# Query units in halves, six more marked rows, an earlier start of the dense products, and VectorE adding V's fourth bank, in a one-core decoder-layer kernel

## Chip, cores and metric

One core of a Trainium2 chip runs the whole kernel. Times are device microseconds of that core. TensorE, VectorE, ScalarE, GpSimd and SyncE each run their own queue of instructions; SyncE and GpSimd issue most of the transfers, which run on 16 transfer engines.

## What is computed

One layer of a decoder, float32, 256 tokens of 2048 channels: an input projection, a convolution group and a sparse attention group, an output projection, a layer norm, then PEER, a layer of single-neuron experts, and a second layer norm. The change touches PEER alone:

```python
def peer(x, w_q, sub_keys, u_tab, v_tab):        # x: 256 tokens x 2048
    q = (xt @ w_q).reshape(n_tok, 8, 2, 128)     # 8 heads, two half queries each
    s = jnp.einsum('nhcd,hckd->nhck', q, sub_keys)
    s1, i1 = lax.top_k(s[:, :, 0], 16)           # 16 of 128 first keys
    s2, i2 = lax.top_k(s[:, :, 1], 16)           # 16 of 128 second keys
    cand_s = s1[..., :, None] + s2[..., None, :]
    cand_i = i1[..., :, None] * 128 + i2[..., None, :]
    top_s, pos = lax.top_k(cand_s, 16)           # 16 of 16384 experts a head
    gates = softmax(top_s)
    h = gelu(einsum('td,thed->the', x, u_tab[experts]), exact)
    return einsum('the,thed->td', gates * h, v_tab[experts])
```

Each token thus needs 8 x 16 = 128 rows of U and of V, 8 KB each.

## The kernel before

**Expert rows.** Tokens lie on 128 partitions, in two tiles of 128. Work goes in 256 numbered *rows* (`ALL`): row s is expert slot s mod 128 of token tile s div 128, a different expert for every partition. GpSimd gathers it (line 512) into one of six places in SBUF, from row 42 (`WIDER_AT`) of seven; a place holds 8 KB of U and 8 KB of V for each partition. Then, row by row:

- VectorE, `dot` (line 1825): the product of the U half with x1 and its sum;
- ScalarE, `gelu` (lines 1266 to 1290): the gelu, the weight (gelu times gate), and the V half times the weight, in two operations of 1024 columns;
- TensorE, `add_turned` (line 880): sixteen transposing products of 128 x 128 that add the scaled V half, turned, into four banks of PSUM; then `y_done` frees the place. From row 248 (`TOKEN_AT`) on, `add_row` (line 891) adds it unturned with a diagonal matrix, in products of 128 x 512, after `turn_back` has turned the banks back.

GpSimd waits for `dots_done` of the row that had the place before it refills the U half, and for `y_done` before the V half.

**Marked rows and dense keys.** Most tokens share some first keys. `popularity` counts them per head, `count` (TensorE, at row 24, `COUNT_AT`) sums over tokens, and `choose` (VectorE, at row 25) takes the 24 most frequent. For these the kernel computes all 128 experts of the key for all tokens: *dense U* is 24 units of 1 MB of U (`dense_part`, line 951), each in four parts, spread over rows 40 to 104 by `DENSE_SLOT`; *dense V* is 24 units of 1 MB of V (`v_dense`, line 993), spread over rows 166 (`VALUES_AT`) to 239 by `VALUE_SLOT`. Between the two, rows 109 to 165 carry the sixteen *chunks* that spread the gates over the dense experts, with two-input operations on VectorE (lines 1850 to 1866).

`mark` (VectorE) gives a row's tokens that use a dense key an id out of bounds, so that the gather skips them; `divide` splits their gates between `row_gate` and `gate`. Rows 32 to 255 (`SPLIT` on) are marked. A marked row is two gathers, one of U halves, then, one row later in GpSimd's queue, one of V halves with the partitions' two halves exchanged. Rows 0 to 31 are not marked and come in one gather of 16 KB a partition. The last two rows have their own ids.

**Query units.** The first heads' queries are made before row 0. The other twelve (`LATER`) half queries come from weight units of 1 MB that SyncE loads (three buffers), each multiplied in three parts (`QUERY_PARTS`, `unit_part`, line 919) in rows 0 to 35, sixteen products of 128 x 256 a unit. ScalarE copies, TensorE scores against the sub-keys (`unit_score`, line 928), ScalarE copies again, VectorE counts the popular keys in the order of `UNIT_ORDER`. Each (tile, head) in `RANKED` takes seven rows (`PACE`) of VectorE steps: the top 16 of both key sets, of their sums, the experts, the gates. The place that is added at row 42 lies where the query weights were, so GpSimd waits there for `unit_scored`.

The order on each engine is written out by the row number in one loop per engine; each engine runs through its own list and waits on semaphores.

Of the kernel before, what the change touches and what calls it, by code (L numbers as in the profile page):

```python
# [11 lines left out]
ALU = mybir.AluOpType  # L12
# [40 lines left out]
WIDER_AT = 42  # L53
# [8 lines left out]
QUERY_PARTS = 3  # L62
# [7 lines left out]
DENSE_ROWS = 65  # L70
DENSE_SLOT = [LATER * QUERY_PARTS + 4 + DENSE_ROWS * m // (DENSE * PARTS) for m in range(DENSE * PARTS)]
# [19 lines left out]
ORDER = BEFORE + [(0, 2), (1, 1), (1, 0), (0, 3)] + RANKED[6:]  # L91
# [15 lines left out]
SPLIT = len(BEFORE) * TOP  # L107
# [4 lines left out]
def layer(nc, xT, x_tok, w_stream, w_kw, w_sub, conv_p, cln, bucket1h, rel_bias,  # L112
          b_out, ln1_col, ln_rows, uv_tab, dense_u, out):
    with ExitStack() as ctx:  # L114
# [180 lines left out]
        key_of = [at_early(f"key_of{c}", [P, TI, SLOTS], 4096 + 1024 * c) for c in range(2)]  # L295
        row_gate = at_early("row_gate", [P, TI, SLOTS], 6144)
# [78 lines left out]
        gates_done, weight_done, parked = sem("gates_done"), sem("weight_done"), sem("parked")  # L375
# [74 lines left out]
        def _(pool):  # L450
# [64 lines left out]
            def place_read(s):  # L515

                pool.wait_ge(y_done, BEFORE_IT[s] + 1)

# [7 lines left out]
            for s in range(ALL):  # L526
                k = PLACE[s]
                i, j = ROW_OF[s]
                if s == 0:
                    pool.wait_ge(first_picked, 1)  # L530
                elif s == 1:
                    pool.wait_ge(picked, 1)
                elif j % TOP == 0 and s < SPLIT:
                    pool.wait_ge(picked, ORDER.index((i, j // TOP)) + 1)
                elif j % TOP == 0:
                    pool.wait_ge(turn_ready, ORDER.index((i, j // TOP)) + 1 - len(BEFORE))
# [27 lines left out]
        def _(pe):  # L564
# [333 lines left out]
            def turn_back(i, banks):  # L898

                for n in banks:  # L900
# [59 lines left out]
            def ids_turn():  # L960

                pe.wait_ge(turn_ready, TI * PH - len(BEFORE))
                pe.wait_ge(gates_done, TI * PH)
# [45 lines left out]
            for s in range(ALL - TAIL):  # L1009
# [40 lines left out]
        def _(act):  # L1050
# [211 lines left out]
            def gelu(s):  # L1262
# [3 lines left out]
                act.activation(dots[:, s:s + 1], dots[:, s:s + 1], ACT.Gelu).then_inc(gelu_done, 1)  # L1266
                if j % TOP == 0:
                    act.wait_ge(gates_done, ORDER.index((i, j // TOP)) + 1)
                act.wait_ge(gelu_done, s + 1)
                if split(s):  # L1270
                    if j % TOP == 0:
                        act.wait_ge(turn_ready, ORDER.index((i, j // TOP)) + 1 - len(BEFORE))
# [39 lines left out]
            def dense_copy(v):  # L1312
# [4 lines left out]
                if v >= EXTRA:  # L1317
                    act.wait_ge(*((picked, v - EXTRA + 1) if RANKED[v - EXTRA] in BEFORE else (turn_ready, ORDER.index(RANKED[v - EXTRA]) + 1 - len(BEFORE))))
# [27 lines left out]
            for s in range(3, ALL):  # L1346
                gelu(s)
                if s % QUERY_PARTS == 0 and 1 <= s // QUERY_PARTS <= LATER:
                    unit_copy(s // QUERY_PARTS - 1)
                if s % QUERY_PARTS == 2 and 1 <= s // QUERY_PARTS <= LATER:  # L1350
                    unit_keys(s // QUERY_PARTS - 1)
# [26 lines left out]
        def _(dve):  # L1378
# [374 lines left out]
            def mark(i, h):  # L1753

                q = i * PH + h
                first, second = (t[:, i, h * TOP:(h + 1) * TOP] for t in key_of)
                dve.scalar_tensor_tensor(out=posf[0][:, :], in0=first, scalar=float(PK), in1=second, op0=ALU.mult, op1=ALU.add)
                wide = [P, TOP, DENSE]
                match = cand_both[:, 0:TOP * DENSE].rearrange("p (r j) -> p r j", j=DENSE)
                link(dve.tensor_tensor(match, first.rearrange("p (r o) -> p r o", o=1).to_broadcast(wide),  # L1760
                                       dense_key[:, :].rearrange("p (o j) -> p o j", o=1).to_broadcast(wide), ALU.is_equal))
                link(dve.tensor_reduce(of_dense[:, :], match, AX.X, ALU.add))
# [5 lines left out]
                link(dve.scalar_tensor_tensor(out=posf[1][:, :], in0=of_dense[:, :], scalar=float(SKIP),  # L1768
                                              in1=posf[0][:, :], op0=ALU.mult, op1=ALU.add))
                turn_ids(i, h)  # L1770

            def divide(i, h):

                g, r = (t[:, i, h * TOP:(h + 1) * TOP] for t in (gate, row_gate))
                link(dve.scalar_tensor_tensor(out=r, in0=of_dense[:, :], scalar=0.5, in1=g, op0=ALU.is_lt, op1=ALU.mult))
                dve.tensor_tensor(g, g, of_dense[:, :], ALU.mult).then_inc(gates_done, 1)
# [26 lines left out]
            def gates_out(r):  # L1803
# [7 lines left out]
                if (i, h) in BEFORE:  # L1811
                    link(dve.tensor_copy(row_gate[:, i, h * TOP:(h + 1) * TOP], g))
                    dve.memset(g, 0.0).then_inc(gates_done, 1)
                elif r >= 4:
                    divide(i, h)
# [11 lines left out]

            def turn_identity():
# [4 lines left out]
            def turn_ids(i, h):  # L1833

                c = i * SLOTS + h * TOP - SPLIT
                cols = slice(c, c + TOP)
                dve.tensor_scalar(u_id[:, cols], posf[1][:, :], 2.0, None, ALU.mult)
                dve.tensor_scalar(v_id[HALF:P, cols], posf[1][0:HALF, :], 2.0, 1.0, ALU.mult, ALU.add)
                dve.tensor_scalar(v_id[0:HALF, cols], posf[1][HALF:P, :], 2.0, 1.0, ALU.mult, ALU.add).then_inc(turn_ready, 1)
                dve.wait_ge(turn_ready, ORDER.index((i, h)) + 1 - len(BEFORE))  # L1840

# [59 lines left out]
            for s in range(ALL - TAIL):  # L1901
                dot(s)
                if s == 0:
# [6 lines left out]
                if r < TI * PH:  # L1910
                    if t == 2:
                        keys_top(r)
                    if t == 3:
                        sums_top(r)
                    if t == 5:
                        hits()
                    if t == 6:
# [13 lines left out]
                for h in range(2, PH):  # L1931
                    u = UNIT_ORDER.index(2 * h)
                    if s == QUERY_PARTS * u + QUERY_PARTS + 3:
# [121 lines left out]
```

## Time and profile before

| | us |
|---|---|
| median of three runs | 1606.35 (1605.69 to 1611.81) |
| the profiled execution | 1601.73 |
| its span | 1599.9 |
| first dot, last dot | 436.4, 1578.4 |
| VectorE busy / TensorE busy / ScalarE busy / GpSimd busy | 1212.1 / 1477.1 / 989.9 / 801.9 |

| from - to, us | what runs |
|---|---|
| 0 - 436 | projections, attention, convolution, first layer norm |
| 453 - 617 | rows 3 to 31, unmarked, with the query units |
| 617 - 654 | rows 32 to 39, marked, with the last query unit |
| 654 - 950 | rows 40 to 104, with dense U |
| 950 - 1199 | rows 105 to 165; the chunks from 1000 us or so |
| 1199 - 1526 | rows 166 to 239, with dense V |
| 1526 - 1600 | last rows, second layer norm, output |

The busy time of TensorE is modelled for pipelined products, so near its full share it does not tell how far the engine is from its limit. The share of the transfer engines is the time that packets took, over sixteen engines; it can pass 1.

### The profile page before, as it was taken

To read this page: it belongs to the slowest core of one execution; us is meant where nothing else is said; L and a number is where in the kernel's file an instruction comes from. 1 tells how busy PE (TensorE), PEld (TensorE's weight loads), DVE (VectorE), ACT (ScalarE), POOL (GpSimd) and SP (SyncE) were. 2 spreads that over 40 slices of the span, in tenths; PEclk is the share of its full clock that TensorE was granted. 3 is DMA by queue.
4 is the path that set the end of the run, shared out by engine and by line. 5 is a ranking of instruction groups with operands and counts; after the bars stand their busy time and mean duration, and the time that the engine had idled before them with its cause. 6 is when DMAs were issued, how large, how long until landed. Compare 5 with 4: busy or idle time off the path is not lost. (4 is left out here: it accounts for less than half of the span.)

```text
span 1599.9 us, 27076 instructions
## 1 busy us (share of the span) xinstructions
PE 1477.1 (92%) x10428; PEld 1343.4 (84%) x10428; DVE 1212.1 (76%) x2091; ACT 989.9 (62%) x1632; POOL 801.9 (50%) x515
## 2 busy tenths in 40 slices
PE   9999999999998779899999997888879989989986
PEld 8999899988887668787899987878868989989973
DVE  5689999775776689978889888888965445445586
ACT  5433345553456557767778677777767657556692
POOL 0000110100123335665667668888888867546883
PEclk9999999999999999999999999888889999999998
DMA  6575544376599999999999999899999999999995
GB/s 258 178 247 182 197 170 154 137 293 233 224 426 426 427 427 418 399 415 394 382 408 418 410 390 368 289 376 384 378 357 394 416 416 412 413 412 403 413 360 198
DMA packets 92977, 543.99 MB, mean 340 GB/s; under 512 B 28274, under 2 KB 28946, under 8 KB 32018
## 3 DMA queue, kind: packets, MB, share of 16 engines
q0 software_dynamic: 71296, 405.11, 63.7%
q1 hardware_dynamic: 20884, 137.00, 22.5%
q8 instruction: 79, 1.29, 0.3%
q14 instruction: 46, 0.38, 0.1%
q10 hardware_dynamic: 672, 0.21, 0.1%
HBM read 682.45 MB, written 4.19 MB: 429 GB/s over the span
## 5 line engine op out<-in xcount | busy, mean ns | idle before, releaser
L512 POOL DMA_INDIRECT uv_row<-in_uv_tab,turned x444 | 710.0, 1599 | 266.1 <-issue 112.2
L1825 DVE CUSTOM_DVE_ANT_0 uv_row<-uv_row,x 128x2048 f32<-128x2048 f32 x256 | 586.8, 2292 | 240.2 <-DMA uv_row<-in_uv_tab,turned 195.1
L1290 ACT ACTIVATE uv_row<-uv_row,turned 128x1024 f32<-128x1024 f32 x432 | 473.1, 1142 | 211.0 <-DMA uv_row<-in_uv_tab,turned 208.4
L880 PE MATMUL psum<-popular,uv_row 128*128 128x128 f32 x3456 | 456.9, 286 | 75.6 <-ACT uv_row L1290 75.2
L880 PEld LDWEIGHTS psum<-popular,uv_row 128*128 128x128 f32 x3456 | 404.0, 148 | 117.0 <-ACT uv_row L1290 108.6
L571 PE MATMUL psum<-xT_hi,w_hi 128*128 128x256 f32 x640 | 183.1, 286 | 3.2 <-DVE w_lo L1410 3.1
L993 PE MATMUL psum<-scratch,dense_unit 128*128 128x128 f32 x1536 | 183.8, 275 | 0.0
L572 PE MATMUL psum<-xT_lo,w_hi 128*128 128x256 f32 x640 | 181.2, 283 | 0.0
L573 PE MATMUL psum<-xT_hi,w_lo 128*128 128x256 f32 x640 | 181.2, 283 | 0.0
L993 PEld LDWEIGHTS psum<-scratch,dense_unit 128*128 128x128 f32 x1536 | 177.6, 192 | 0.0
L951 PE MATMUL psum<-x1T,dense_unit 128*128 128x256 f32 x768 | 176.6, 379 | 0.0
L1065 ACT ACTIVATE w_hi<-w_raw 128x2048 fp32r<-128x2048 f32 x62 | 118.7, 1915 | 85.6 <-DMA w_raw<-in_w_stream 85.6
L1410 DVE TENSOR_TENSOR w_lo<-w_raw,w_hi 128x2048 fp32r<-128x2048 f32 x62 | 141.6, 2286 | 28.7 <-ACT w_hi L1065 27.8
L951 PEld LDWEIGHTS psum<-x1T,dense_unit 128*128 128x128 f32 x768 | 141.0, 190 | 16.3
L1275 ACT ACTIVATE turned<-dots,row_gate 64x1 f32<-64x1 f32 x444 | 129.8, 292 | 11.0 <-issue 0.4
L571 PEld LDWEIGHTS psum<-xT_hi,w_hi 128*128 128x128 f32 x640 | 122.8, 192 | 7.0 <-issue 3.1
L572 PEld LDWEIGHTS psum<-xT_lo,w_hi 128*128 128x128 f32 x640 | 122.9, 192 | 0.1
L573 PEld LDWEIGHTS psum<-xT_hi,w_lo 128*128 128x128 f32 x640 | 122.8, 192 | 0.0
L512 POOL DMA_INDIRECT uv_row<-in_uv_tab,eid x32 | 52.3, 1634 | 114.1 <-PE psum L880 96.7
L1266 ACT ACTIVATE dots<-dots 128x1 f32<-128x1 f32 x256 | 48.9, 191 | 67.3 <-DVE dots L1825 67.0
L880 PE MATMUL psum<-ident,uv_row 128*128 128x128 f32 x512 | 66.9, 281 | 24.6 <-ACT uv_row L1290 24.6
L880 PEld LDWEIGHTS psum<-ident,uv_row 128*128 128x128 f32 x512 | 57.4, 144 | 34.9 <-ACT uv_row L1290 34.0
(281 smaller groups left out, 1712.8 us busy)
## 6 DMA issues: line engine op xcount, KB each, us to landing
w_raw<-in_w_stream SPq DMA_DIRECT2D x63, 1024.0 KB, 4.8
dense_unit<-in_dense_u SPq DMA_DIRECT2D x24, 1024.0 KB, 8.9
dense_unit<-in_uv_tab SPq DMA_DIRECT2D x24, 1024.0 KB, 9.3
wq_first<-in_w_stream SPq DMA_DIRECT2D x8, 1024.0 KB, 12.6
uv_row<-in_uv_tab,turned POOLq DMA_INDIRECT x444, 19.1
wq_third<-in_w_stream SPq DMA_DIRECT2D x4, 1024.0 KB, 11.8
xT_raw<-in_xT SPq DMA_DIRECT2D x4, 512.0 KB, 5.4
turned_rows<-dist_row POOLq DMA_DIRECT2D x1, 2048.0 KB, 14.3
```

Of the source, the lines that this page charges most:

```text
L512: pool.indirect_dma_start(dst, None, tab, bass.IndirectOffsetOnAxis(ap=ids, axis=0), bounds_check=tab.shape[0] - 1, oob_is_err=False).then ...
L571: pe.matmul(dst, a[0], b[0], start=first, stop=False)
L572: pe.matmul(dst, a[0], b[1], start=False, stop=False)
L573: return pe.matmul(dst, a[1], b[0], start=False, stop=last)
L880: last = pe.matmul(bank(i, b // 4)[:, b % 4 * P:(b % 4 + 1) * P], row[k][:, D + b * P:D + (b + 1) * P], order[:, :], is_transpose=True, st ...
L951: last = pe.matmul(side[v % 2][:, 0:S], w[:, c, :], x1T[:, c, :], start=c == 0, stop=c == KC - 1)
L993: last = pe.matmul(bank(i, n)[:, b % 4 * P:(b % 4 + 1) * P], dense_unit[v % 2][:, b * P:(b + 1) * P], mixed[:, v, i * P:(i + 1) * P], star ...
L1065: act.activation(w_hi[k], w_raw[k], ACT.Copy).then_inc(hi_done, 1)
L1275: whole = act.activation(weight_turned[to, c:c + 1], dots[of, s:s + 1], ACT.Identity, scale=row_gate[of, i, j:j + 1])
L1290: act.activation(v, v, ACT.Identity, scale=w).then_inc(scaled, 1)
L1410: dve.tensor_tensor(w_lo[k], w_raw[k], w_hi[k].bitcast(F32), ALU.subtract).then_inc(lo_dve, 1)
L1825: dve.tensor_tensor_reduce(row[k][:, 0:D], row[k][:, 0:D], x1[:, ROW_OF[s][0], :], 1.0, 0.0, ALU.mult, ALU.add, dots[:, s:s + 1]).then_inc ...
```

## The change

- `QUERY_PARTS` 3 to 2: query units in halves, in rows 1 to 24; the calls that belong to them move accordingly, and `unit_score` now stands ahead of `unit_part` in TensorE's row. `WIDER_AT` 42 to 36.
- `COUNT_AT` 24 to 18: keys are chosen at row 19; `UNIT_ORDER` brings the units that count forward. The chosen keys are the same.
- `SPLIT` 32 to 26: the last six slots of head (0, 1) are marked as well; `mark` and `divide` take a first slot j. The marks of (0, 1), (1, 0), (0, 2) follow at rows 19, 20 and 21.
- `DENSE_ROWS` 65 to 78, start at row 27 instead of 40: dense U ends at row 104 as before.
- In rows 166 to 247 (`ADDED`) TensorE adds twelve blocks, not sixteen, ScalarE scales 1024 + 512 columns, and VectorE adds the fourth bank, weighted, into `y_last` in SBUF (`add_last`), behind the next row's dot. GpSimd waits for it as well before it refills the place. TensorE adds `y_last` once, at row 248.

```diff
-WIDER_AT = 42
+WIDER_AT = 36
...
-QUERY_PARTS = 3
+QUERY_PARTS = 2
...
-DENSE_ROWS = 65
-DENSE_SLOT = [LATER * QUERY_PARTS + 4 + DENSE_ROWS * m // (DENSE * PARTS) for m in range(DENSE * PARTS)]
+DENSE_ROWS = 78
+DENSE_SLOT = [LATER * QUERY_PARTS + 3 + DENSE_ROWS * m // (DENSE * PARTS) for m in range(DENSE * PARTS)]
...
-UNIT_ORDER = [4, 5, 6, 8, 10, 12, 14, 7, 9, 11, 13, 15]
+UNIT_ORDER = [4, 6, 8, 10, 5, 12, 14, 7, 9, 11, 13, 15]
-COUNT_AT = 24
+COUNT_AT = 18
...
-SPLIT = len(BEFORE) * TOP
+LATE = 10
+ADDED = range(VALUES_AT, TOKEN_AT)
+SPLIT = TOP + LATE
...
             def place_read(s):
                 pool.wait_ge(y_done, BEFORE_IT[s] + 1)
+                if BEFORE_IT[s] in ADDED:
+                    pool.wait_ge(y_last_done, ADDED.index(BEFORE_IT[s]) + 1)
...
-                    for b in range(8 * half, 8 * half + 8):
+                    for b in range(8 * half, 12 if half and s in ADDED else 8 * half + 8):
...
+                    if i == 1 and n == 3:
+                        pe.wait_ge(y_last_done, len(ADDED))
+                        last = pe.matmul(bank(1, 3), ident_turned[:, :], y_last[:, :], start=False, stop=True, skip_group_check=True)
...
-                if s < LATER * QUERY_PARTS:
-                    unit_part(s // QUERY_PARTS, s % QUERY_PARTS)
-                if s >= QUERY_PARTS + 1 and s % QUERY_PARTS == 1 and s // QUERY_PARTS <= LATER:
-                    unit_score(s // QUERY_PARTS - 1)
+                if s >= 4 and s % QUERY_PARTS == 0 and (s - 4) // QUERY_PARTS < LATER:
+                    unit_score((s - 4) // QUERY_PARTS)
+                if 1 <= s <= LATER * QUERY_PARTS:
+                    unit_part((s - 1) // QUERY_PARTS, (s - 1) % QUERY_PARTS)
...
-                    v = row[PLACE[s]][:, D + half * DC:D + (half + 1) * DC]
+                    v = row[PLACE[s]][:, D + half * DC:D + (DC + 512 if half and s in ADDED else (half + 1) * DC)]
...
+            def add_last(s):
+                k, n, c = PLACE[s], ADDED.index(s), split_col(s)
+                dve.wait_ge(weight_done, s + 1)
+                dve.wait_ge(v_half_in[k], v_half_from[k] + 16 * SPLIT_USES[s])
+                if n:
+                    dve.wait_ge(y_last_done, n)
+                dve.scalar_tensor_tensor(out=y_last[:, :], in0=row[k][:, D + 3 * 512:2 * D], scalar=weight_turned[:, c:c + 1],
+                                         in1=y_last[:, :], op0=ALU.mult, op1=ALU.add).then_inc(y_last_done, 1)
...
                 dot(s)
+                if s == VALUES_AT:
+                    link(dve.memset(y_last[:, :], 0.0))
+                if s - 1 in ADDED:
+                    add_last(s - 1)
...
                 if s == CHOSEN_AT:
                     choose()
                     turn_identity()
+                    mark(0, 1, LATE)
+                    divide(0, 1, LATE)
+                if s == CHOSEN_AT + 1:
+                    mark(1, 0)
+                    divide(1, 0)
+                if s == CHOSEN_AT + 2:
                     mark(0, 2)
                     divide(0, 2)
-                if s == CHOSEN_AT + 3:
-                    mark(1, 0)
-                    divide(1, 0)
```

## Rows read from the trace of the kernel before

**Rows 1.** The page: rate in 40 slices, and the group of ScalarE's scaling.
```profile
GB/s 258 178 247 182 197 170 154 137 293 233 224 426 426 427 427 418 399 415 394 382 408 418 410 390 368 289 376 384 378 357 394 416 416 412 413 412 403 413 360 198
...
L1290 ACT ACTIVATE uv_row<-uv_row,turned 128x1024 f32<-128x1024 f32 x432 | 473.1, 1142 | 211.0 <-DMA uv_row<-in_uv_tab,turned 208.4
```

**Rows 2.** Table by stage: length, five engines' busy us, TensorE clock, DMA share, GB/s.
```profile
453.00:617.00 164.00, 138.16 (x851) 119.97 (x851) 120.28 (x301) 95.23 (x151) 52.90 (x33) 0.99 1.01 426
617.00:654.00 37.00, 32.84 (x222) 29.11 (x221) 34.29 (x79) 28.59 (x51) 20.28 (x14) 1.00 1.00 407
654.00:950.00 296.00, 283.44 (x1789) 254.16 (x1790) 257.13 (x611) 221.80 (x377) 196.35 (x137) 0.99 1.00 404
...
1040.00:1199.00 159.00, 133.69 (x957) 124.03 (x958) 128.81 (x127) 111.88 (x196) 135.83 (x77) 0.86 0.97 373
1199.00:1526.00 327.00, 313.05 (x2703) 301.76 (x2702) 170.40 (x148) 215.79 (x378) 233.44 (x156) 0.99 1.01 410
```

**Rows 3.** The same table for shorter stretches (columns PE, PEld, DVE, ACT, POOL).
```profile
740.00:800.00 60.00, 58.45 (x379) 53.19 (x380) 54.67 (x131) 47.66 (x82) 39.23 (x27) 1.00 0.98 382
820.00:900.00 80.00, 80.00 (x523) 73.51 (x522) 71.86 (x177) 64.28 (x109) 54.46 (x39) 1.00 1.01 416
980.00:1040.00 60.00, 54.58 (x428) 51.21 (x427) 53.01 (x55) 44.94 (x77) 52.70 (x24) 0.92 0.86 303
...
520.00:580.00 60.00, 48.91 (x298) 40.93 (x296) 41.39 (x96) 33.73 (x54) 19.93 (x11) 1.00 1.01 427
```

**Rows 4.** Queue 0: whole kernel, 654 to 950 us, 1199 to 1526 us.
```profile
q0 software_dynamic: 71296, 405.11, 63.7%
...
q0 software_dynamic: 19484, 96.19, 81.1%
...
q0 software_dynamic: 22075, 110.50, 83.6%
```

**Rows 5.** Waits, 654 to 950 us: total us, times, longest.
```profile
POOL uv_row L512 <- PE psum L880: 44.1, 29, 3.2
...
ACT scratch L1319 <- PE psum L951: 29.4, 12, 4.1
...
DVE gsum L1808 <- ACT gate L1260: 18.6, 7, 3.6
...
DVE uv_row L1825 <- DMA uv_row<-in_uv_tab,turned: 9.3, 5, 3.1
```

**Rows 6.** Timeline of TensorE, 760 to 800 us: start, us, line.
```profile
773.42 3.62 PE L951 MATMUL psum<-x1T,dense_unit 128*128 128x256 f32 x16
776.88 1.91 PE L880 MATMUL psum<-popular,uv_row 128*128 128x128 f32 x16
778.62 1.89 PE L951 MATMUL psum<-x1T,dense_unit 128*128 128x256 f32 x8
```

**Rows 7.** Waits, 1199 to 1526 us.
```profile
DVE uv_row L1825 <- DMA uv_row<-in_uv_tab,turned: 156.5, 73, 4.8
...
POOL uv_row L512 <- PE psum L880: 42.8, 27, 3.4
...
POOL uv_row L512 <- DVE dots L1825: 11.3, 5, 2.8
```

**Rows 8.** Line 512, gathers issued in three stretches: ns min/median/max.
```profile
L512 POOL DMA_INDIRECT uv_row<-in_uv_tab,turned x137: 984/991/3071, 653.7 to 947.5; - x137
...
L512 POOL DMA_INDIRECT uv_row<-in_uv_tab,turned x156: 984/991/3088, 1198.7 to 1525.8; - x156
...
L512 POOL DMA_INDIRECT uv_row<-in_uv_tab,turned x11: 1686/2965/3049, 998.9 to 1026.1; - x11
```

**Rows 9.** Line 1889, VectorE's last-norm operation, ns min/median/max.
```profile
L1889 DVE SCALAR_TENSOR_TENSOR x<-x,rstd,ln_rows_sb x8: 746/746/753, 1558.8 to 1595.9; 128x512 f32<-128x512 f32 x8
```

**Rows 10.** Timelines of TensorE and GpSimd near the end.
```profile
1563.67 24.20 PE L891 MATMUL psum<-uv_row,scratch 128*128 128x512 f32 x56
...
1556.82 2.69 POOL L512 DMA_INDIRECT uv_row<-in_uv_tab,turned  x1 [0.31 <-issue]
```

More of the change, by code:

```diff
@@ L374, in layer @@
             sem(n) for n in ("chunk_ready", "chunk_done", "chunk_mixed", "v_dense_done"))
-        gates_done, weight_done, parked = sem("gates_done"), sem("weight_done"), sem("parked")
+        gates_done, weight_done, parked, y_last_done = (sem(n) for n in ("gates_done", "weight_done", "parked", "y_last_done"))
         row2_done, row2_copied = sem("row2_done"), sem("row2_copied")
@@ L532, in _ @@
                     pool.wait_ge(picked, 1)
-                elif j % TOP == 0 and s < SPLIT:
-                    pool.wait_ge(picked, ORDER.index((i, j // TOP)) + 1)
+                elif s == TOP:
+                    pool.wait_ge(picked, 2)
+                elif s == SPLIT:
+                    pool.wait_ge(turn_ready, 1)
                 elif j % TOP == 0:
-                    pool.wait_ge(turn_ready, ORDER.index((i, j // TOP)) + 1 - len(BEFORE))
+                    pool.wait_ge(turn_ready, RANKED.index((i, j // TOP)))
                 if k == 4 and s < PLACES:
@@ L1266, in gelu @@
                 act.activation(dots[:, s:s + 1], dots[:, s:s + 1], ACT.Gelu).then_inc(gelu_done, 1)
+                r = RANKED.index((i, j // TOP))
                 if j % TOP == 0:
-                    act.wait_ge(gates_done, ORDER.index((i, j // TOP)) + 1)
+                    act.wait_ge(gates_done, r + 1 if r < 2 else r + 2)
+                elif s == SPLIT:
+                    act.wait_ge(gates_done, 3)
                 act.wait_ge(gelu_done, s + 1)
                 if split(s):
-                    if j % TOP == 0:
-                        act.wait_ge(turn_ready, ORDER.index((i, j // TOP)) + 1 - len(BEFORE))
+                    if s == SPLIT or j % TOP == 0:
+                        act.wait_ge(turn_ready, max(r, 1))
                     c = split_col(s)
@@ L1317, in dense_copy @@
                 if v >= EXTRA:
-                    act.wait_ge(*((picked, v - EXTRA + 1) if RANKED[v - EXTRA] in BEFORE else (turn_ready, ORDER.index(RANKED[v - EXTRA]) + 1 - len(BEFORE))))
+                    r = v - EXTRA
+                    act.wait_ge(*((picked, r + 1) if RANKED[r] in BEFORE else (turn_ready, r)))
                 act.activation(mixed[:, BLOCK_OF[v], :], side[v % 2][:, 0:S], ACT.Gelu).then_inc(dense_copied, 1)
@@ L1347, in _ @@
                 gelu(s)
[L1348 to L1351, printed above, removed]
+                if s >= 3 and s % QUERY_PARTS == 1 and (s - 3) // QUERY_PARTS < LATER:
+                    unit_copy((s - 3) // QUERY_PARTS)
+                if s >= 5 and s % QUERY_PARTS == 1 and (s - 5) // QUERY_PARTS < LATER:
+                    unit_keys((s - 5) // QUERY_PARTS)
                 r, t = s // PACE + 1, s % PACE
@@ L1751, in experts, with mark @@
                                              in1=pick[1][:, j:], op0=ALU.mult, op1=ALU.add).then_inc(picked, 1)
-            def mark(i, h):
+            def mark(i, h, j=0):
                 q = i * PH + h
[L1756 to L1759, printed above, removed]
+                n = TOP - j
+                first, second = (t[:, i, h * TOP + j:(h + 1) * TOP] for t in key_of)
+                ids, of = posf[0][:, 0:n], of_dense[:, 0:n]
+                dve.scalar_tensor_tensor(out=ids, in0=first, scalar=float(PK), in1=second, op0=ALU.mult, op1=ALU.add)
+                wide = [P, n, DENSE]
+                match = cand_both[:, 0:n * DENSE].rearrange("p (r j) -> p r j", j=DENSE)
                 link(dve.tensor_tensor(match, first.rearrange("p (r o) -> p r o", o=1).to_broadcast(wide),
                                        dense_key[:, :].rearrange("p (o j) -> p o j", o=1).to_broadcast(wide), ALU.is_equal))
-                link(dve.tensor_reduce(of_dense[:, :], match, AX.X, ALU.add))
+                link(dve.tensor_reduce(of, match, AX.X, ALU.add))
                 if q == TI * PH - 1:
@@ L1767, in mark, with divide @@
                         link(dve.tensor_scalar(last_id[:, a, :], last_f[:, :], 2.0, float(a), ALU.mult, ALU.add))
[L1768 to L1776, printed above, removed]
+                link(dve.scalar_tensor_tensor(out=posf[1][:, 0:n], in0=of, scalar=float(SKIP), in1=ids, op0=ALU.mult, op1=ALU.add))
+                turn_ids(q * TOP + j - SPLIT, n, RANKED.index((i, h)))
+            def divide(i, h, j=0):
+                g, r = (t[:, i, h * TOP + j:(h + 1) * TOP] for t in (gate, row_gate))
+                of = of_dense[:, 0:TOP - j]
+                if j:
+                    dve.memset(gate[:, i, h * TOP:h * TOP + j], 0.0)
+                link(dve.scalar_tensor_tensor(out=r, in0=of, scalar=0.5, in1=g, op0=ALU.is_lt, op1=ALU.mult))
+                dve.tensor_tensor(g, g, of, ALU.mult).then_inc(gates_done, 1)
             def popularity(i, h):
@@ L1831, in turn_identity, with turn_ids @@
                 link(dve.tensor_copy(ident_turned[:, HALF:P], ident[:, 0:HALF]))
[L1833 to L1840, printed above, removed]
+            def turn_ids(c, n, ready):
+                cols, ids = slice(c, c + n), posf[1]
+                dve.tensor_scalar(u_id[:, cols], ids[:, 0:n], 2.0, None, ALU.mult)
+                dve.tensor_scalar(v_id[HALF:P, cols], ids[0:HALF, 0:n], 2.0, 1.0, ALU.mult, ALU.add)
+                dve.tensor_scalar(v_id[0:HALF, cols], ids[HALF:P, 0:n], 2.0, 1.0, ALU.mult, ALU.add).then_inc(turn_ready, 1)
+                dve.wait_ge(turn_ready, ready)
             def chunk_keys(c, half):
@@ L1914, in _ @@
                         sums_top(r)
+                    if t == 4:
+                        hits()
                     if t == 5:
-                        hits()
-                    if t == 6:
                         experts(r)
```

13 lines of the change are left out of this document (8 added, 5 removed).

## The prediction, made before the result was known

> **What bounds the kernel now.** I read the rate in the page's 40 us slices first [rows 1]. From 440 us to 1560 us, the whole stage of the expert rows, it shows where the transfers are short of their best: 427 GB/s at first, 418 to 382 in the middle, 289 in the slice at 1000 us, 357 to 394 until 1240, then 403 to 416. A table by stage [rows 2] adds how busy the transfer engines were: DMA share 1.01, 1.00, 1.00, 0.97, 1.01. So the gather stage is bound by transfers, and a change there is worth what it takes from the bytes or gives back of the rate, and nothing else.
>
> The rate needs a yardstick, so I cut out stretches in which nothing disturbs the transfers [rows 3]: whole 16 KB rows run at 427 GB/s (520 to 580 us), half rows at 416 (820 to 900). Beside them stand 382 GB/s (740 to 800), where TensorE is busy 58.5 of 60 us, and 303 GB/s (980 to 1040), where GpSimd is busy 52.7 of 60 us issuing the gathers. Then I asked who waits for whom while dense U runs [rows 5]: VectorE waits for a landing in only 9.3 of 296 us, GpSimd waits 44.1 us for TensorE to free a place, and ScalarE waits 29.4 us for a dense product. With VectorE busy 257.1 and TensorE 283.4 of 296 us [rows 2], three resources are nearly full at once there. While dense V runs it is different: VectorE waits for landings 156.5 of 327 us [rows 7] and is busy only 170.4 [rows 2].
>
> **The change, part by part.**
>
> *Six more rows marked.* Rows 26 to 31 become two half gathers that skip the tokens of the 24 dense keys. A whole row is 128 x 16 KB = 2.10 MB, at 427 GB/s 4.91 us. For a marked row I divide what queue 0 moved [rows 4] by the gathers issued meanwhile [rows 8], two to a row: 96.19 MB / 68.5 = 1.40 MB while U runs, 110.50 / 78 = 1.42 while V runs. From above, all of queue 0's 405.1 MB less 32 whole rows (67.1 MB) over 224 marked rows is 1.51 MB, and that still holds other transfers. I take 1.45 MB, 69% of a row, 3.49 us at 416 GB/s. Saved 1.42 us a row, times 6: **8.5 us**; at 1.40 and 1.51 MB it is 9.2 and 7.7. What a single head skips may lie outside both; I allow 7 to 11. Six more gathers on GpSimd (0.99 to 3.1 us each [rows 8]) lie beside the transfers: that engine is busy 52.9 of 164 us before row 32 [rows 2]. One more marking on VectorE and one memset, some 2.5 us by my estimate from the short operations of that stage, and all first markings now stand in rows 19 to 21 instead of 25 and 28. VectorE is busy 120.3 of 164 us there, and five more rows are in flight behind the one it works on. I take 0; if the cover is gone, 3 us once.
>
> *Query units in halves.* The same 12 MB of weights and the same products, in 24 rows instead of 36. Transfers: 4.91 us for the row plus half a unit (0.52 MB, 1.23 us) make 6.1 us a row. TensorE: eight products instead of 5.3. Sixteen records take 1.73 us more than eight, so a product of two records takes 0.43 us, and sixteen transposes are followed by the next work after 1.74 us [rows 6]; with 0.2 for the scores that is 3.5 + 1.7 + 0.2 = 5.4 us. Transfers stay the longer, and the bytes move earlier, not away: 0, at worst 2 us of missed overlap. GpSimd's wait for the last unit's scores moves with the seventh place from row 42 to 36; the scores are then made at TensorE's row 26, ten rows ahead of that gather, so the wait should vanish. The stage at 617 to 654 us, which holds it, still ran at DMA share 1.00 and 407 GB/s [rows 2], so at most 1 us comes back.
>
> *Dense U from row 27 to 104 instead of 40 to 104.* The bytes stay. Per row TensorE now has 96 / 78 = 1.23 quarter units instead of 1.48. A quarter is 8 records, 1.73 us [rows 6], so 1.74 + 2.14 = 3.9 us a row instead of 1.74 + 2.57 = 4.3. The transfers of such a row: 3.49 us plus 24 / 78 of a 1.05 MB unit (0.78 us) = 4.3 us, where they were 4.4. TensorE is then 0.4 us clear of them instead of 0.1, and what it cost can come back: the stage moved 404 GB/s x 296 us = 119.6 MB, at 416 GB/s 287.5 us, so 8.5 us were lost. But VectorE stays: its 257.1 us busy and 18.6 us waiting for the gates' exponentials [rows 5] are 4.2 us a row. I take half: **4 us**, between 0 and 8.5. Behind row 105 nothing moves: the same chunks in the same rows, with GpSimd held between VectorE's operations as now (135.8 of 159 us busy [rows 2]).
>
> *V's fourth bank on VectorE, rows 166 to 247.* TensorE loses 4 of 16 transposes (0.44 us a row), ScalarE scales 1536 columns instead of two times 1024, which take 1.14 us each [rows 1] (some 0.55 us less). VectorE gains one 128x512 operation; the nearest row has the same shape and both inputs in SBUF, 0.75 us [rows 9]. 82 x 0.75 = 61 us on VectorE, of which some 75 rows in the stage: 170 + 56 = 226 of 327 us. Its waits for landings (156 us) take that in. The new wait stands behind a dot: the weight and the V half of the row before. What is queued behind it is the next dot, whose U half is issued after that V half, so it would not have run earlier; GpSimd waits additionally for the sum before it refills a V place. The relief on TensorE is off the path: the stage moves 410 GB/s, its middle slices 416 to 412 [rows 1, 2], 3 us at most. I take 0, from -3 to +8 (below).
>
> *The end.* TensorE's last chain is 56 records in 24.2 us from 1563.7 us on [rows 10], 0.43 us a record; the product that adds the VectorE sum is 2 more, +0.9 us on the path. It starts behind ScalarE's scaling of row 247 (now 0.55 less) and sixteen transposes (now 0.4 less). VectorE meanwhile runs dots back to back with GpSimd's gathers tied to them (2.69 us each [rows 10]); seven additions of 0.75 us push these by up to 5 us, of which I put about 3 down as covered, since ScalarE too must finish those rows first. I take **+1 us**, -1 to +4.
>
> Sum: -8.5 - 4 + 0 + 1 = **-11.5 us**. The profiled execution took 1601.7 us (a span of 1599.9 and 1.8 around it), so 1590.2. The median of the three runs is 1606.35 (one was 1611.8), 0.3% above it; on that scale 1594.9, so I forecast **1595 us**, -0.7%. A measurement of this kernel can tell about 0.5%, 8 us, from no change: the marked rows alone are about that much, which is why the sign of the small terms matters.
>
> **A rule that speaks against it.** When a gather is issued while nothing on VectorE stands in its way it takes 0.99 us; between 1000 and 1028 us, where dots and two-input operations follow each other, eleven took 1.69 to 3.05, median 2.97, and the rate fell to 303 GB/s [rows 3, 8]. The Trainium skill (SBUF — State Buffer, "SBUF: two separate sides") states it: VectorE and GpSimd share a port pair that is locked for a whole instruction, and a VectorE operation with two SBUF inputs takes it against a GpSimd operation that reads SBUF. The trace agrees. The new addition has two SBUF inputs.
>
> **Rivals.**
>
> 1. *Slower: GpSimd becomes the bound while dense V runs.* Each gather may have to wait out the new 0.75 us. GpSimd has 42.8 + 11.3 = 54 us of waits for places in 327 us [rows 7], 0.7 us a row. One such wait a row (61 us) is just hidden; from there on each further 0.1 us costs 8 us. Price: if the stage falls to the 373 GB/s of the chunk stage [rows 2], 134 MB take 359 us, +32, in all 1627; at 390 GB/s +17 (344 us), 1612. Against it: VectorE would be busy 69% of this stage, and 81% in the chunk stage; it idles over a microsecond a row, and an undisturbed gather needs 1.0. Chance 0.10.
>
> 2. *VectorE holds dense U's stage.* It has 276 us of work and waits in 296; with the rows from 27 on as fast as 4.2 us it would be full, so no rate comes back, the marking burst costs 3, and the end costs 2: -8.5 + 5 = -3.5, 1603. For it: only 9.3 us of waiting for landings. Against: the gate wait is itself a wait for ScalarE, which waited 29.4 us for dense products. Chance 0.22.
>
> 3. *All of the rate comes back.* TensorE's relief restores 416 GB/s while U runs and 3 us while V runs: -8.5 - 8.5 - 3 = -20, 1586. Chance 0.13.
>
> 4. *The marking does not shorten anything*, since the transfers wait for places before row 32 already: then only the 4 us remain and the end costs its 1: 1603. The share of 1.01 at 426 GB/s [rows 2] speaks against it. Chance 0.05.
>
> The forecast's own case, 1590 to 1600, has 0.50. The range takes in rival 3 and rivals 2 and 4 and leaves out the slow one and the far ends: 1585 to 1607. Faster by over 0.5% (below 1598.3): the forecast's case but for its upper edge (0.46) and rival 3 with its further end, 0.13, and a little of rival 2, 0.05: 0.64. Within 0.5%: the upper edge of the forecast, most of rival 2, rival 4 and the mildest of rival 1, 0.27. Slower: 0.09.
>
> **What would show it.** After the change, rows 26 to 31 should land a microsecond or more apart faster than rows 3 to 25, queue 0 should carry some 401 MB (6 x 0.65 less), the stage of dense U should run at 408 GB/s or more with TensorE busy below 90%, and GpSimd should have no wait for the scores near row 36. While dense V runs the rate should be 405 to 415 GB/s, with VectorE's wait for landings down to about 100 us and gathers whose median stays near 1 us. Wrong would be: rate there below 400 with GpSimd never waiting for a place (rival 1); dense U at 404 or less with VectorE above 90% busy (rival 2); TensorE's last chain starting later against the last landing than now.

## The result and the profile after

The changed kernel takes 1600.5 us (median of 15 runs), the one before 1608.1 in the same sessions: ratio **0.9945, interval 0.9929 to 0.9961**, -8.8 us by the ratio. Forecast were 1595 us and -11.5. Ratios leave out executions that took over 1.5% more than the fastest of their kernel: one of `e2_v_alone` (1670 us), one of `g1_later_and_40` (2858 us) and one of the kernel before (2436 us). A single execution moves by several microseconds (1593 to 1605 for the changed kernel, 1603 to 1614 for the other), so two profiles alone don't show this difference: the profiled spans are 1600.8 and 1599.9 us, and already row 0 starts 2.7 us later in the profile after. So I compare lengths from dot to dot within the stage, over several variants.

| us between dots of rows | 3-24 | 24-32 | 32-40 | 40-105 | 105-166 | 166-240 | 240 to end |
|---|---|---|---|---|---|---|---|
| before | 124.3 | 44.3 | 32.2 | 296.6 | 248.8 | 326.8 | 73.9 |
| after | 130.7 | 37.4 | 34.7 | 290.4 | 251.2 | 326.0 | 74.5 |

Rows 24 to 32 and 40 to 105 are shorter; rows 3 to 24 give 6.4 us back. Such a length is not yet a gain or a loss: a stage also gets shorter when more of its bytes were moved before its first dot. Rate times length tells the two apart. These are the rows of the stage table from the dot of row 3 to that of row 105 and from row 40 to row 105, first of the kernel before, then of the changed one:

```profile
453.30:950.50 497.20, 454.64 (x2864) 403.50 (x2863) 411.87 (x990) 346.13 (x579) 269.54 (x183) 0.99 1.01 411
654.00:950.50 296.50, 283.94 (x1793) 254.66 (x1794) 257.56 (x613) 222.30 (x377) 196.35 (x137) 0.99 1.00 404
...
456.00:949.20 493.20, 455.40 (x2871) 405.26 (x2869) 413.21 (x1000) 347.51 (x581) 272.71 (x188) 0.99 1.00 410
658.80:949.20 290.40, 264.54 (x1705) 234.51 (x1703) 255.10 (x606) 221.63 (x371) 188.58 (x131) 0.99 1.00 402
```

Rows 40 to 105 took 6 us less because 3 MB less were moved in them (404 GB/s x 296.5 us = 119.8 MB, 402 x 290.4 = 116.7), not because the rate rose. From row 3 to row 105 the rate is the same too, and 4 us are gone with 2 MB.

The stage table of the changed kernel, for the stretches that answer to [rows 2] (rows 3 to 31, 32 to 39, 40 to 104, most of the chunks, dense V; columns as there):

```profile
456.00:624.00 168.00, 159.98 (x981) 143.42 (x980) 126.73 (x319) 100.73 (x168) 59.86 (x42) 0.98 1.01 424
624.00:659.00 35.00, 31.08 (x191) 27.54 (x190) 31.55 (x77) 25.32 (x45) 24.48 (x17) 0.95 1.02 416
659.00:949.00 290.00, 264.34 (x1703) 234.31 (x1701) 254.87 (x605) 221.35 (x369) 188.38 (x131) 0.99 1.00 402
1040.00:1200.00 160.00, 135.64 (x960) 124.94 (x958) 128.15 (x127) 110.50 (x194) 137.14 (x76) 0.86 0.96 365
1200.00:1526.00 326.00, 286.14 (x2391) 274.56 (x2392) 220.93 (x222) 184.65 (x378) 236.10 (x153) 0.97 1.01 408
```

TensorE fell from 283.4 of 296 us to 264.3 of 290 while U runs, and yet the rate is 402 GB/s, no better than 404 before. The waits of that stretch, which answer to [rows 5], point to the reason:

```profile
POOL uv_row L514 <- PE psum L886: 33.4, 17, 3.6
ACT dots L1275 <- DVE dots L1845: 27.4, 22, 3.2
POOL uv_row L514 <- DVE dots L1845: 26.3, 9, 3.6
...
DVE gsum L1825 <- ACT gate L1269: 20.1, 8, 4.3
ACT scratch L1332 <- PE psum L960: 7.4, 8, 2.0
...
DVE uv_row L1845 <- DMA uv_row<-in_uv_tab,turned: 0.9, 1, 0.9
```

VectorE waits 0.9 us for landings in 290 us, where it was 9.3. ScalarE now waits for VectorE's dots (27.4 us, before 1.4) and hardly for dense products (7.4, before 29.4). VectorE does not wait for rows, then: the data is there. What it waits for is the exponential of the gates, 20.1 us in 8 waits.

While V runs the waits answer to [rows 7]:

```profile
ACT uv_row L1302 <- DMA uv_row<-in_uv_tab,turned: 136.0, 70, 5.2
DVE uv_row L1845 <- DMA uv_row<-in_uv_tab,turned: 74.8, 63, 3.5
...
POOL uv_row L514 <- PE psum L886: 40.9, 26, 3.5
...
DVE y_last L1855 <- issue: 21.7, 17, 2.3
...
POOL uv_row L514 <- DVE y_last L1855: 3.9, 6, 2.4
```

VectorE's wait for landings fell from 156.5 to 74.8 us, and 21.7 us more pass idle before the additions; in all it is idle 105 of 326 us, where it was 157 of 327. That took the additions in. GpSimd still waits for places, and its gathers of the stage took 1.54 us in the mean, 1.51 before. Queue 0 carries 3.1 MB less, and the addition costs what its nearest row said [rows 4, 9]:

```profile
q0 software_dynamic: 72160, 401.97, 63.6%
...
L1855 DVE SCALAR_TENSOR_TENSOR y_last<-uv_row,turned,y_last x82: 740/747/773, 1207.0 to 1558.6; 128x512 f32<-128x512 f32 x82
```

### The profile page after: what moved, and what is told of

It is laid out like the page before. It is cut to its first block, busy times and chain, and to the rows that moved or that the text cites. A ratio compares the mean times of both kernels' runs of the same rounds, so it can differ in the third digit from the quotient of the medians.

```text
span 1600.8 us, 26707 instructions
## 1 busy us (share of the span) xinstructions
PE 1456.6 (91%) x10102; PEld 1322.7 (83%) x10102; DVE 1269.8 (79%) x2183; ACT 959.7 (60%) x1638; POOL 811.0 (51%) x521
## 4 chain that ended last, share of the span: by engine, by line
DMA 24%; DVE 17%; PE 6%; issue 6%; ACT 5%; POOL 4%; POOLq 0%; DVEq 0%; ACTq 0%
DMA uv_row<-in_uv_tab,turned 24%; DVE uv_row L1845 10%; POOL uv_row L514 4%; PE psum L886 3%; ACT uv_row L1302 3%; PE psum L897 1%; PE psum L1002 1%; ACT L1269 1%; PE psum L989 1%; DVE scratch L1675 0%; DVE first_key L1879 0%; ACT turned L1287 0%; DVE key_of L1759 0%; DVE idx L1681 0%; DVE idx L1674 0%
## 5 line engine op out<-in xcount | busy, mean ns | idle before, releaser
L514 POOL DMA_INDIRECT uv_row<-in_uv_tab,turned x456 | 729.8, 1600 | 273.6 <-issue 121.1
L1302 ACT ACTIVATE uv_row<-uv_row,turned 128x1024 f32<-128x1024 f32 (+1 forms) x444 | 451.1, 1063 | 220.8 <-DMA uv_row<-in_uv_tab,turned 216.5
L886 PE MATMUL psum<-popular,uv_row 128*128 128x128 f32 x3224 | 435.8, 289 | 117.7 <-ACT uv_row L1302 116.8
L886 PEld LDWEIGHTS psum<-popular,uv_row 128*128 128x128 f32 x3224 | 380.2, 148 | 163.6 <-ACT uv_row L1302 155.7
L1002 PE MATMUL psum<-scratch,dense_unit 128*128 128x128 f32 x1536 | 188.7, 280 | 0.0
L1002 PEld LDWEIGHTS psum<-scratch,dense_unit 128*128 128x128 f32 x1536 | 182.8, 197 | 0.0
L960 PE MATMUL psum<-x1T,dense_unit 128*128 128x256 f32 x768 | 180.1, 381 | 0.0
L514 POOL DMA_INDIRECT uv_row<-in_uv_tab,eid x26 | 38.7, 1490 | 98.2 <-PE psum L886 81.0
L1495 DVE SCALAR_TENSOR_TENSOR scratch<-glu_sb,conv_sb,scratch 128x256 f32<-128x256 f32 x203 | 82.6, 473 | 0.0
L487 POOL TENSOR_TENSOR scratch<-scratch,convT 128x256 f32<-128x256 f32 x6 | 16.5, 2745 | 130.3 <-DVE convT L1499 130.3
```

What stands on the lines that cost most here:

```text
L514: pool.indirect_dma_start(dst, None, tab, bass.IndirectOffsetOnAxis(ap=ids, axis=0), bounds_check=tab.shape[0] - 1, oob_is_err=False).then ...
L960: last = pe.matmul(side[v % 2][:, 0:S], w[:, c, :], x1T[:, c, :], start=c == 0, stop=c == KC - 1)
L1002: last = pe.matmul(bank(i, n)[:, b % 4 * P:(b % 4 + 1) * P], dense_unit[v % 2][:, b * P:(b + 1) * P], mixed[:, v, i * P:(i + 1) * P], star ...
```

## The experiments

All ratios are against the kernel before, run on the same chip in the same session. Stage lengths are from one profile each. Rows 40 to 105 repeat within 2 us (290.4 to 292.1 in the four profiles with the changed kernel's work there: `after`, `e1_no_v`, `e3_six_whole`, `f5_add_twice`). Behind row 105 the scatter is larger: rows 105 to 166, where no two kernels differ, took 243.7 to 254.7 us, rows 166 to 240 took 325.8 to 334.9.

**The parts.** Four kernels take one part out, or do one alone.

*Without V's bank* (`e1_no_v`; the memset and the product that adds `y_last` go with it):

```diff
-ADDED = range(VALUES_AT, TOKEN_AT)
+ADDED = range(0)
```

> The changed kernel with V's fourth bank given back to TensorE and ScalarE; the rest of the change stays. The changed kernel stands at 0.9945 of the one before (-8.8 us). Theory of the forecast (the stage of dense V is bound by transfers, the bank costs 1 us at the end): 0.994, 1598 to 1600 us beside 1608. Rival 1 (VectorE's addition holds up the gathers and costs several us in rows 166 to 247): 0.991 or less. Rival 3 (TensorE's relief gives back rate while V runs): 0.996 or more.

Measured 0.9956 (0.9936 to 0.9975). *V's bank alone, on the kernel before* (`e2_v_alone`: `ADDED`, `add_last`, the twelve blocks, the shorter scaling, the wait in `place_read`, the memset and the last product, nothing else):

> The kernel before with V's fourth bank on VectorE and nothing else. Theory of the forecast: 1.000 to 1.001 (0 to +2 us), the stage of rows 166 to 239 within 2 us of 327. Rival 1: 1.003 or more, with gathers issued later and the rate below 405 GB/s. Rival 3: 0.998, the stage 3 us shorter.

Measured 0.9973 (0.9954 to 0.9991). So the bank is worth -1.8 us in the one pair, with an error of 4, and -4.3 in the other, with an error of 3. The stage of dense V itself doesn't show it above its scatter: 326.8 us before and 332.2 with the bank alone, 330.3 without it and 326.0 with it in the changed kernel. The first pair is the forecast's value within its error, the second is at rival 3's; neither leaves room for rival 1.

*The six rows whole again* (`e3_six_whole`; keys still chosen at row 19):

```diff
-SPLIT = TOP + LATE
+SPLIT = 2 * TOP
...
-                    mark(0, 1, LATE)
-                    divide(0, 1, LATE)
+                    dve.sem_inc(turn_ready, 1)
+                    dve.memset(gate[:, 0, TOP:2 * TOP], 0.0).then_inc(gates_done, 1)
```

> The changed kernel with rows 26 to 31 gathered whole and unmarked as before; keys are still chosen at row 19 and dense U still starts at row 27. Theory of the forecast (bytes at the transfers' rate: 8.5 us): 0.9945 + 0.0053 = 0.9998, some 1608 us, queue 0 back at 405 MB. Rival (transfers wait for places there, marks shorten nothing): 0.994 to 0.996.

Measured 1.0020 (0.9995 to 1.0045), 1607.6 us, queue 0 at 405.11 MB. The marking carries the gain: 0.0075 between the two, 12 us, with an error of some 5. Rows 24 to 32 took 44.3 us here at 423 GB/s and 37.4 in the changed kernel at 416, that is 18.7 and 15.6 MB; the 3.1 MB are what queue 0 lost. Over all variants profiled those rows took 44.3 to 45.8 us unmarked (five) and 34.6 to 37.6 marked (nine), some 8 us apart, near the term of the sum. Without the marking the rest of the change is no gain.

*Dense U from row 40 again* (`e4_dense_from_40`):

```diff
-DENSE_ROWS = 78
-DENSE_SLOT = [LATER * QUERY_PARTS + 3 + DENSE_ROWS * m // (DENSE * PARTS) for m in range(DENSE * PARTS)]
+DENSE_ROWS = 65
+DENSE_SLOT = [LATER * QUERY_PARTS + 16 + DENSE_ROWS * m // (DENSE * PARTS) for m in range(DENSE * PARTS)]
```

> The changed kernel with dense U spread over rows 40 to 104 again; the marked rows, the query units in halves and V's bank stay. Theory of the forecast (4 us of rate come back by the spreading, between 0 and 8.5): 0.997, some 1604 us, with 380 to 405 GB/s while U runs. Rival 2 (VectorE holds that stage, spreading gives nothing): 0.9945, no different from the changed kernel.

Measured 0.9941 (0.9917 to 0.9964): the spreading brings nothing that shows; a gain of 4 us would lie at the edge of the error. Rows 40 to 105 took 286.9 us with all 24 units inside, 290.4 with the spread, both at 402 GB/s. Its row of the stage table and two of its waits:

```profile
657.00:944.00 287.00, 280.49 (x1780) 254.42 (x1781) 255.21 (x606) 221.05 (x374) 183.05 (x130) 0.99 1.00 402
```
```profile
ACT scratch L1332 <- PE psum L960: 39.5, 16, 4.1
...
DVE gsum L1825 <- ACT gate L1269: 21.3, 9, 3.2
```

TensorE is as full as it was before the change, ScalarE waits for its products as before, and the rate is the same 402 GB/s. TensorE was late, and that cost no rate.

*Query units in halves alone* (`f1_halves_alone`, on the kernel before: `QUERY_PARTS = 2` with the calls that move, `WIDER_AT = 36`; keys still at row 25, dense U from row 40):

> The kernel before with the query units in halves and the seventh place from row 36, nothing else: keys chosen at row 25, rows 0 to 31 whole, dense U from row 40. The traces so far show two sides of this. Rows 3 to 24 took 130 to 131 us with units in halves and 124 to 125 in thirds; rows 40 to 105 took 287 to 292 us with them and 295 to 297 in thirds, where GpSimd stood 8.9 us at row 42 and was then only 2 to 3 rows ahead. New theory (the stage of dense U is bound by VectorE when its rows are there, and the stall is what made it wait): both show, +6 and -6 to -9, total 0.996 to 1.001. Forecast's theory (bytes only move, the stall costs at most 1 us): 1.000 to 1.001, rows 40 to 105 unchanged at 295 us or more.

Measured 1.0015 (0.9995 to 1.0035). Rows 3 to 24 took 129.6 us (124.3 in thirds), rows 40 to 105 290.9 (296.6). The two are one thing seen twice, as the rows of the stage table from row 3 to row 105 and from row 40 to row 105 show (those of the kernel before are above):

```profile
452.90:950.00 497.10, 457.61 (x2864) 411.66 (x2863) 411.58 (x990) 346.35 (x579) 267.75 (x183) 0.97 1.00 412
659.10:950.00 290.90, 281.34 (x1793) 254.40 (x1794) 257.27 (x613) 223.11 (x380) 190.70 (x132) 0.99 1.00 403
```

Rows 40 to 105 ran at 403 GB/s, 404 in the kernel before: the 5.6 us that they are shorter are some 2.5 MB that were moved ahead of row 40, where they cost as much. Up to row 105 both kernels take 497 us.

The stall at row 42 goes with the same edit. In the kernel before GpSimd stands there 8.9 us, with the place whose memory the query weights hold, and is then, from row 37 to row 48, only 3 or 4 rows ahead of VectorE, where `f1_halves_alone` has 5 or 6. Its wait in the stretch 628 to 665 us, and the same stretch in `f1_halves_alone`:

```profile
POOL uv_row L512 <- PE psum L928: 8.9, 1, 8.9
```
```profile
POOL uv_row L512 <- issue: 5.8, 19, 0.3
POOL uv_row L512 <- PE psum L880: 0.3, 1, 0.3
```

The lost lead looks dear in rows 40 to 105 and is not: it is bytes that come later, and the 497 us show no price for the stall. No run moves the place alone.

**Who is the bound from row 40 to 105?** Two kernels add work there, one takes a wait away. `f2_vector_more` and `f3_tensor_more` add, per row:

```diff
+                if 40 <= s < 105:
+                    link(dve.tensor_reduce(dense_count[:, 0:1], iota_f[:, :], AX.X, ALU.add))
```
```diff
+                if 40 <= s < 105:
+                    pe.matmul(ps[0][:, 0:S], x1T[:, 0, 0:P], x1T[:, 0, :], start=True, stop=True)
```

> The changed kernel with one more VectorE operation (a sum over 256 columns, some 0.42 us, its result unused) in each of rows 40 to 104. New theory (VectorE is the bound there): nearly its whole price shows, 65 x 0.45 = 29 us, 1625 to 1630 us, rows 40 to 105 in 315 to 320 us. Forecast's theory (transfers and TensorE are the bound): under 8 us.

> The changed kernel with one more product of 128 x 256 (0.43 us, its result unused) on TensorE in each of rows 40 to 104, 28 us of work. New theory (VectorE is the bound): 0 to 6 us. If TensorE still decides there: 20 us or more.

Measured 1.0080 (1.0050 to 1.0111) and 0.9973 (0.9946 to 1.0000), against 0.9945 without either. Their rows of the stage table, VectorE's first:

```profile
655.00:962.00 307.00, 274.13 (x1697) 239.94 (x1695) 279.12 (x670) 221.11 (x370) 205.34 (x131) 0.97 0.97 383
```
```profile
654.00:945.00 291.00, 284.06 (x1819) 256.21 (x1818) 254.80 (x605) 220.07 (x370) 189.18 (x131) 1.00 1.00 400
```

24 us more of VectorE's work lower the rate from 402 to 383 GB/s and make the stage 17 us longer (290.4 to 307.5 us from dot to dot) and the kernel 22 us slower, with an error of some 5; 20 us more of TensorE's make the stage 1 us longer and the kernel 4.5 us slower with about the same error. So VectorE is the bound of the changed kernel there, though not for its full price: I had written 29 us.

*The gates taken up one row later* (`f4_gates_later`), so that ScalarE's exponential is done when VectorE comes for it:

```diff
-                if t == 0 and 1 <= r - 1 < TI * PH:
+                if (t == 1 if 4 <= r - 1 < TI * PH - 1 else t == 0) and 1 <= r - 1 < TI * PH:
```

> The changed kernel with VectorE taking up the gates of the fifth to fifteenth ranked head one row later, so that it no longer waits for ScalarE's exponential (20.1 us in 8 waits between rows 40 and 105). New theory (VectorE is the bound): rows 40 to 105 fall from 290 us towards 119 MB at 416 GB/s, 280 to 284 us, total 0.989 to 0.992. Forecast's theory (bound by transfers): within 2 us of the changed kernel, 0.9945.

Measured 0.9924 (0.9896 to 0.9952), rows 40 to 105 in 285.3 us. Its waits and its stage row:

```profile
656.00:942.00 286.00, 262.53 (x1677) 232.24 (x1676) 255.74 (x608) 219.66 (x371) 203.01 (x130) 0.99 1.01 406
```
```profile
DVE uv_row L1845 <- DMA uv_row<-in_uv_tab,turned: 16.3, 12, 3.6
...
DVE gsum L1825 <- ACT gate L1269: 1.3, 2, 1.1
```

19 us of waiting for ScalarE are gone, 5 us come off the stage, at 406 GB/s instead of 402, and 15 us turn up as waits for landings: right behind VectorE stand the transfers. The step 0.9945 to 0.9924 lies within the two intervals; the stage's length and the waits are what show it.

The same edit on the kernel before (`h1_before_gates_later`; there the gates of head (1, 1) are divided with another head's marks, because those are made in between, so the output is wrong; the work is the same):

> The kernel before with VectorE taking up the gates of the fifth to fifteenth ranked head one row later, nothing else. There VectorE waited 18.6 us for the exponentials in rows 40 to 105, but TensorE was busy 283 of 296 us and held places back 44 us. If VectorE alone were the bound, it gains as in the changed kernel: rows 40 to 105 at 288 to 291 us, ratio 0.995 to 0.998. If TensorE is as late as VectorE there (dense U in 65 rows and the stall at row 42), within 2 us: 0.999 to 1.001.

Measured 0.9982 (0.9965 to 0.9999), but rows 40 to 105 stayed at 296.6 us. VectorE's wait for the gates fell from 18.6 to 7.4 us and its wait for landings rose from 9.3 to 18.6. So in the kernel before the rows themselves were late in that stage, VectorE was not its bound alone, and what the total gained I can't place.

**Does the addition hold up the gathers?** `f5_add_twice` makes it twice, the first time with weight 0:

```diff
+                link(dve.scalar_tensor_tensor(out=y_last[:, :], in0=row[k][:, D + 3 * 512:2 * D], scalar=0.0,
+                                              in1=y_last[:, :], op0=ALU.mult, op1=ALU.add))
```

> The changed kernel with VectorE's addition of V's fourth bank made twice in rows 166 to 247 (the extra one with weight 0, same operands), 82 x 0.75 = 61 us more work with two SBUF inputs. In the changed kernel VectorE still waits 74.8 us for landings there, and only 6 gathers met the addition (mean 1.36 us instead of 0.99). Forecast's theory (landings' waits take it in, the gathers are hardly held): rows 166 to 239 in 326 to 336 us, total at most +6 us on the changed kernel, ratio 0.995 to 0.998. Rival 1 (the port lock makes GpSimd the bound): 15 us or more, ratio 1.003 or more, GpSimd without a wait for a place, rate below 400 GB/s.

Measured 0.9975 (0.9951 to 0.9999), rows 166 to 240 in 328.6 us. The stage, and two waits:

```profile
1193.00:1522.00 329.00, 288.56 (x2393) 277.49 (x2392) 268.87 (x296) 184.23 (x377) 221.15 (x154) 0.96 1.01 410
```
```profile
POOL uv_row L514 <- PE psum L886: 55.3, 33, 4.8
...
DVE uv_row L1845 <- DMA uv_row<-in_uv_tab,turned: 37.7, 33, 3.7
```

Twice the additions, and GpSimd still waits for places, 55.3 us instead of 40.9, at the same 410 GB/s; a gather of the stage took 1.44 us in the mean, 1.54 in the changed kernel. Rows 240 to 248 took 34.4 us instead of 30.0 (27.3 without the addition): most of what the total lost.

**The fastest.** `g1_later_and_40` joins the later gates and dense U from row 40; `h2_best_no_v` takes V's bank out of it.

> The changed kernel with VectorE taking up the gates one row later (0.9924 by itself) and dense U spread over rows 40 to 104 again (0.9941 by itself). If in rows 40 to 105 both VectorE's waits and the transfers are near the bound: spreading dense U from row 27 keeps 13 rows' share of bytes out of that stage, so this should be no better than the gates alone: rows 40 to 105 in 287 to 292 us, but rows 3 to 40 shorter by some 3 us; 0.991 to 0.995. If the early bytes only cost: 0.990 or less.

> The fastest variant so far (gates one row later, dense U from row 40; 0.9903) with V's fourth bank given back to TensorE and ScalarE. The two pairs so far put the bank on VectorE at -1.8 us (changed kernel) and -4.3 us (alone on the kernel before), each within 3 to 4 us. If that gain is real: ratio 0.992 to 0.993. If it is nothing: 0.990 to 0.991.

Measured 0.9903 (0.9872 to 0.9934), 1594.6 us, and 0.9909 (0.9889 to 0.9928), 1593.9 us. By the ratio both beat the kernel before by some 15 us, by the medians by 10 and 13, and they are the fastest measured; from the changed kernel (0.9929 to 0.9961) the second is just clear, the first overlaps it by a hair. Against `f4_gates_later` alone, rows 3 to 40 took 197.9 us instead of 201.1 in the first, rows 40 to 105 287.8 instead of 285.3, and rows 3 to 105 485.7 instead of 486.4: spreading dense U from row 27 moves bytes from the one stretch to the other and neither gains nor clearly costs. V's bank is -1 us in this pair, with an error of some 6. Over the three pairs, weighted by their errors, it is 3 us gained, give or take 2; only the pair on the kernel before (0.9954 to 0.9991) is clear of nothing by itself, and narrowly.

## Why the prediction came out as it did

- **Six more rows marked, -8.5 us: right in mechanism, oversized in bytes.** Rows 24 to 32 are 7 to 8 us shorter, and taking the marks back costs 12 us with an error of 5. Queue 0 lost 3.14 MB, 0.52 a row, where I had 0.65, so these six rows skip only a quarter of their tokens. That is 6.8 us by the rates of [rows 3], and the 3.1 MB between `e3_six_whole` and the changed kernel in rows 24 to 32 took 6.9. What the 12 us hold beyond that, if not chance, I can't assign. The sign that I had set, rows 26 to 31 a microsecond closer to each other than rows 3 to 25, told nothing: these six took 28.4 us and the 23 ahead of them 139.7, but 29.0 and 139.5 in the kernel before, where they were not marked.
- **Query units in halves, 0: right.** The forecast was that "the bytes move earlier, not away", and they did: rows 3 to 24 took 5 to 6 us longer, rows 40 to 105 as much less, and up to row 105 the time is the same 497 us. The wait at row 42 vanished as forecast, and "at most 1 us comes back" holds too.
- **Dense U from row 27, -4 us: wrong.** The failed step is "at 416 GB/s 287.5 us, so 8.5 us were lost", with TensorE as the one who lost them, and half of the gap taken as gain without a row behind it. TensorE busy 264.3 of 290 us or 280.5 of 287, the rate was 402 GB/s both times, where 408 or more was the sign I had set. In the changed kernel VectorE freed places no faster; its 276 us of work and gate waits stood in my own text as rival 2. In the kernel before the runs name no single bound: 11 us less of gate waits left the stage at 296.6 us. Relief for TensorE moved a wait from one engine to another (29.4 us of ScalarE's to 7.4, and 1.4 us for dots to 27.4). The premise ahead of it, that the whole gather stage is bound by transfers because their share reads 1.00, failed with it: in rows 40 to 105 the share is 1.00 too, and VectorE's operations set the time.
- **V's bank, 0 us: right within its range, -3 to +8; the pairs say some 3 us gained.** The added work went where the wait for landings was, 156.5 to 74.8 us (forecast: about 100). Rival 1 fell: its condition was one wait of 0.75 us a row; 7 of 153 gathers of the stage were issued while an addition ran, and took 1.30 us in the mean.
- **The end, +1 us: right.** The additions push rows 240 to 248 by 2.7 us (30.0 instead of 27.3), and what follows takes that back: 74.5 us instead of 73.9 from row 240 on. The product that adds the sum is there with the 0.86 us between its start and that of the last chain, and that chain has the same 24.2 us [rows 10]:

```profile
1563.73 1.02 PE L917 MATMUL psum<-y_last,popular 128*128 128x512 f32 x2
1564.59 24.20 PE L897 MATMUL psum<-uv_row,scratch 128*128 128x512 f32 x56
```

So the sum came near partly by luck: dense U's 4 us did not come and the marking brought some 2 us less by its bytes, and V's bank brought some 3 that I had put at nothing. The 2.7 us between forecast and measurement are within the error of the measurement and could not have told these apart; only the variants do. Rival 2 gave 1603 us because it let the marking burst and the end cost 5 us; those did not show. On dense U it had the mechanism right, with 22 in 100, and the forecast's case had it wrong.

## What to carry to other kernels

Where a stage's transfers run at 97% of their best rate, first ask which engine never waits for a landing, and test it by adding work to each suspect; here relief for another engine that merely looked full was worth nothing. Before a shorter stage is called a gain, multiply its rate by its length: with the same rate and fewer bytes it was not sped up, and if the kernel's bytes are the same in all, another stage has grown by as much. A sum of several small terms that comes out right says little about the terms; take each out by itself.

## What the runs showed of the hardware

The hold between VectorE and GpSimd goes by the operation in progress. Six of the seven gathers that were issued while the addition ran, with two inputs in SBUF, ended 0.86 to 0.87 us after the addition's end; the seventh, issued 0.05 us after the addition's start, took its undisturbed 0.99 us. A gather that waits for a dot does not wait for the addition behind it (1545.50 + 3.03 us is 0.86 us after the dot's end at 1547.67, though the addition ran from 1547.60). And one issued in the midst of a two-input operation that reads one input from PSUM took its undisturbed 0.99 us, though 0.68 us of the operation were left. Timelines of GpSimd and VectorE in the changed kernel:

```profile
1212.28 0.99 POOL L514 DMA_INDIRECT uv_row<-in_uv_tab,turned  x1 [0.30 <-issue]
...
1256.37 1.25 POOL L514 DMA_INDIRECT uv_row<-in_uv_tab,turned  x1 [0.31 <-issue]
...
1545.50 3.03 POOL L514 DMA_INDIRECT uv_row<-in_uv_tab,turned  x1 [0.30 <-issue]
...
1184.61 0.99 POOL L514 DMA_INDIRECT uv_row<-in_uv_tab,turned  x1 [0.30 <-issue]
```
```profile
1212.23 0.77 DVE L1855 SCALAR_TENSOR_TENSOR y_last<-uv_row,turned,y_last 128x512 f32<-128x512 f32 x1 [1.11 <-ACT turned L1287]
...
1256.01 0.75 DVE L1855 SCALAR_TENSOR_TENSOR y_last<-uv_row,turned,y_last 128x512 f32<-128x512 f32 x1 [2.10 <-issue]
...
1545.38 2.29 DVE L1845 CUSTOM_DVE_ANT_0 uv_row<-uv_row,x 128x2048 f32<-128x2048 f32 x1
...
1547.60 0.75 DVE L1855 SCALAR_TENSOR_TENSOR y_last<-uv_row,turned,y_last 128x512 f32<-128x512 f32 x1
...
1184.31 0.98 DVE L1895 TENSOR_TENSOR scratch<-scratch,psum 128x384 f32<-128x384 f32 x1 [0.86 <-PE psum L989]
```

This fits the small cost of doubling the additions: a gather pays for the rest of one operation, not for a chain of them. The Trainium skill (SBUF — State Buffer, "Who interferes with whom") names two SBUF inputs as a condition under which an operation contends with GpSimd's reads; the trace agrees. It shows besides that the hold passes to a waiting gather at the end of an operation.
